# A two-layer decoder trunk in one kernel: order of the work between the first norm and the expert loop

## What is computed

```python
h = layer_norm(DN_ALPHA * h + mix, ln1_g[l], ln1_b[l])        # (xf - mu) * rsqrt(var + EPS) * g + b
scores = jax.nn.sigmoid(xf @ w_router)                        # 272 tokens (16 meta, 256 real), 64 experts
# sel = scores + bias; best 4 of 8 groups by their two best sums; best 8 experts of these
gates = gates / gates.sum(-1, keepdims=True) * ROUTE_SCALE
routed = sum over the chosen experts: gate * (silu(x @ w_gate) * (x @ w_up)) @ w_down
shared = (jax.nn.silu(xf @ ws_gate) * (xf @ ws_up)) @ ws_down
h = layer_norm(DN_ALPHA * h + routed + shared, ln2_g[l], ln2_b[l])
```

## Time and profile before

| | |
|---|---|
| device time, median of 3 runs | 1487.34 us |
| lowest and highest | 1483.96, 1491.04 us |
| profiled execution, span from first to last instruction | 1480.7 us |
| TensorE matmul busy | 1430.7 us, 97% |
| VectorE busy | 353.0 us, 24% |
| ScalarE busy | 254.0 us, 17% |
| GpSimd busy | 138.3 us, 9% |

### The profile page before, as it was taken

The page is one execution under the profiler, slowest core; times in us unless marked ns, Lnnn a source line. Parts: engine busy times, 40 slices in busy tenths (PEclk is TensorE's granted clock), DMA queues, the critical chain, the costliest instruction groups (busy, mean ns, idle before and its releaser), DMA issues. The chain is left out here.

```text
span 1480.7 us, 21355 instructions
## 1 busy us (share of the span) xinstructions
PE 1430.7 (97%) x8428; PEld 739.1 (50%) x8428; DVE 353.0 (24%) x1093; ACT 254.0 (17%) x608; POOL 138.3 (9%) x169
## 2 busy tenths in 40 slices
PE   8999999999999999999979999999999999999996
PEld 4755544444544454445437654444544554554552
DVE  0444551111111111111143435511111111111112
ACT  1243201111111111111122441011111111111110
POOL 2032111000000000000000221100000000000000
PEclk9999999999999999999989999999999999999998
DMA  9722429999999999999935224299999999999990
GB/s 331 299 97 86 172 78 380 409 407 396 400 400 402 394 400 407 406 393 399 346 139 199 94 106 171 78 388 405 410 417 415 412 413 414 409 413 414 413 398 33
DMA packets 103489, 471.66 MB, mean 319 GB/s; under 512 B 11744, under 2 KB 18080, under 8 KB 70544
## 3 DMA queue, kind: packets, MB, share of 16 engines
q1 hardware_dynamic: 91344, 442.32, 75.1%
q0 software_dynamic: 12096, 28.70, 5.5%
HBM read 484.91 MB, written 3.35 MB: 330 GB/s over the span
## 5 line engine op out<-in xcount | busy, mean ns | idle before, releaser
L614 PE MATMUL bank<-ring,region 128*64 128x256 f32 x4096 | 456.0, 381 | 1.7 <-issue 1.7
L614 PEld LDWEIGHTS bank<-ring,region 128*64 128x64 f32 x4096 | 296.9, 138 | 176.2 <-issue 39.7
L573 PE MATMUL bank<-region 128*128 128x512 f32 x512 | 267.5, 607 | 1.4 <-ACTq L1322 0.7
L652 PE MATMUL bank<-ring,region 128*64 128x512 f32 x1024 | 249.6, 608 | 2.4 <-ACT region L1141 1.4
L1532 DVE TENSOR_TENSOR region<-region,bank 128x256 f32<-128x256 f32 x64 | 27.0, 421 | 560.2 <-ACT region L1134 560.2
L1141 ACT ACTIVATE region<-bank 128x512 f32<-128x512 f32 x128 | 76.4, 597 | 474.6 <-PE bank L652 474.6
L1830 POOL DMA_INDIRECT region<-h_rows,rank_i x64 | 63.7, 995 | 919.7 <-DVE region L1511 863.8
L652 PEld LDWEIGHTS bank<-ring,region 128*64 128x64 f32 x1024 | 62.3, 136 | 162.9 <-issue 86.5
L573 PEld LDWEIGHTS bank<-region 128*128 128x128 f32 x512 | 78.1, 191 | 58.1 <-issue 54.9
L586 PEld LDWEIGHTS bank<-const,region 128*128 128x128 f32 x512 | 66.9, 195 | 69.2 <-ACT region L1125 42.7
L1134 ACT ACTIVATE region<-bank 128x256 f32<-128x256 f32 x64 | 24.6, 385 | 413.8 <-PE bank L614 413.8
(11 more groups left out here) (206 smaller groups left out, 847.6 us busy)
## 6 DMA issues: line engine op xcount, KB each, us to landing
ring<-in_w_gate_dram SPq DMA_DIRECT2D x64, 2048.0 KB, 10.4
ring<-in_w_up_dram SPq DMA_DIRECT2D x64, 2048.0 KB, 13.0
ring<-in_w_down_dram SPq DMA_DIRECT2D x64, 2048.0 KB, 9.1
ring<-in_w_in_dram SPq DMA_DIRECT2D x8, 2048.0 KB, 17.4
ring<-in_w_o_dram SPq DMA_DIRECT2D x4, 2048.0 KB, 11.0
ring<-in_w_in_dram SPq DMA_DIRECT2D x4, 1024.0 KB, 8.2
ln_par<-in_ln_g_dram POOLq DMA_DIRECT2D x4, 512.0 KB, 5.5
ln_par<-in_ln_b_dram POOLq DMA_DIRECT2D x4, 512.0 KB, 7.4
```

The costliest lines, as they stand in the source:

```text
L573: last = mm(bank[SUM_BANKS[n][half]][0:w, :], selg[:, u, t0:t0 + w], y_sb[:, u, half * 512:(half + 1) * 512], start=False, stop=stop, skip ...
L614: last = mm(bank[5][64 * e:64 * e + 64, part * F:(part + 1) * F], xgT[:, u, kk, 64 * e:64 * e + 64], w[:, e, kk, :], start=(kk == 0), stop ...
L652: last = mm(bank[6][64 * e:64 * e + 64, :], mo["h2"][:, j * 128 + 64 * e:j * 128 + 64 * e + 64], w[:, e, j, half * 512:(half + 1) * 512], ...
```

## The change

- `finish` moves from VectorE to GpSimd, for all chunks of the first norm. It stands there right behind the powers and ahead of the clearing of `score`.
- `xg` is cleared by ScalarE, as a copy of constants with scale 0, behind its last router sigmoid; a new semaphore, `rows_clear`, tells GpSimd. `moe_clear` now counts `score` alone.
- VectorE makes all eight list steps at once (`first_lists`), with `wait_ge` where `hold_here` stood, ahead of the maximum count and of all shared hidden values. These come in `round_`, behind `read_lists`.
- TensorE turns the lists ahead of opening the sums. Down product of chunk 1 stays ahead of the loop; those of chunk 2 and, in layer 0, chunk 0 go in four pieces into the first pair, where the scatters are in the others. `scattered` is raised by the last piece.

```diff
@@ -574,7 +575,7 @@
                               start=False, stop=stop, skip_group_check=True)
                 return last
 
-            def round_(l, r):
+            def round_(l, r, shared_piece=None):
 
                 g = l * ROUNDS + r
                 past = pe.snap(rounds_run)
@@ -625,11 +626,15 @@
                             pe.wait_ge(y_ready, g * 64 + p * 2)
                             pe.wait_ge(selg_ready, g * 32 + p)
                             scatter(l, 1 - u, 1, 0)
+                        elif shared_piece:
+                            shared_piece(0)
                         if not ends:
                             pe.wait_ge(xta_ready, g * 32 + p + 2)
                             turn_x(1 - u, 1)
                         if not opens:
                             scatter(l, 1 - u, 1, 1)
+                        elif shared_piece:
+                            shared_piece(1)
                         pe.wait_ge(h_ready, g * 32 + p + 1)
                         if not ends:
                             pe.wait_ge(xtb_ready, g * 32 + p + 2)
@@ -640,6 +645,8 @@
                             scatter(l, 1 - u, 2, 0)
                             if l == 0:
                                 scatter(l, 1 - u, 0, 0)
+                        elif shared_piece:
+                            shared_piece(2)
                         pe.wait_ge(ht_ready, g * 32 + p + 1)
                         pe.wait_ge(slot_in[base + 2], arrived)
                         w = ring[:, base + 2, :].rearrange("p (e j n) -> p e j n", e=2, j=2)
@@ -655,6 +662,8 @@
                             last.then_inc(y_done, 1)
                             if half == 0 and not opens:
                                 scatter(l, 1 - u, 2, 1).then_inc(scattered, 1)
+                            elif half == 0 and shared_piece:
+                                shared_piece(3).then_inc(scattered, 1)
 
                 two_pairs(0, first=True)
                 with pe.Fori(1, PAIRS // 2 - 1) as i:
@@ -1019,38 +1028,46 @@
                             mm(bank[b][:, :], k["alpha"], h_tok[:, n, half * 512:(half + 1) * 512], start=True, stop=False,
                                skip_group_check=True)
 
-                def shared_down(n):
+                def shared_down(n, pieces):
+
                     t0, w = CHUNKS[n]
                     pe.wait_ge(shared_ready, SHARED[l][n])
-                    if n == 0:
-                        parts = [(o, q * 256, 256) for q, o in enumerate(meta_quads(SUM_BANKS[0][0], 256))]
-                    else:
-                        parts = [(bank[b][0:w, :], half * 512, 512) for half, b in enumerate(SUM_BANKS[n])]
-                    for j in range(2):
+                    for at in pieces:
+                        if n == 0:
+                            j, parts = at, [(o, q * 256, 256) for q, o in enumerate(meta_quads(SUM_BANKS[0][0], 256))]
+                        else:
+                            j, half = at // 2, at % 2
+                            parts = [(bank[SUM_BANKS[n][half]][0:w, :], half * 512, 512)]
                         for o, c0, cols in parts:
                             last = mm(o, hsT[:, j, t0:t0 + w], wsd[:, j, c0:c0 + cols], start=False, stop=False,
                                       skip_group_check=True)
                     return last
 
+                pe.wait_ge(score_ready, SCORED[l])
+                if l == 0:
+                    pe.wait_ge(shared_sig, SHARED[l][0])
+                turn_lists(l * ROUNDS)
                 pe.wait_ge(h_ready_tok, NORM[(l, 0)][2])
-                pe.wait_ge(ws_down_in, l * 16 + 16)
                 open_sums(1)
                 turn_hidden(1)
                 open_sums(2)
                 turn_hidden(2)
-                shared_down(1)
-                pe.wait_ge(score_ready, SCORED[l])
-                turn_lists(l * ROUNDS)
+                pe.wait_ge(ws_down_in, l * 16 + 16)
+                shared_down(1, range(4))
                 if l == 0:
                     turn_hidden(0)
                     open_sums(0)
-                last = shared_down(2)
-                if l == 0:
-                    last = shared_down(0)
-                last.then_inc(scattered, 1)
                 hold_here(pe, count_ready, l + 1)
                 most = pe.value_load(count_i[0:1, 0:1], min_val=0, max_val=T)
-                round_(l, 0)
+                pe.wait_ge(shared_ready, SHARED[l][QUERIES[l][0] if l == 0 else 2])
+
+                def shared_piece(at):
+                    last = shared_down(2, [at])
+                    if l == 0 and at >= 2:
+                        last = shared_down(0, [at - 2])
+                    return last
+
+                round_(l, 0, shared_piece)
                 last_sums(l, 0, sums_done, SUMMED[l][SUM_ORDER[l][-1]])
                 with pe.If(most > CAP):
                     with pe.Fori(1, ROUNDS) as r:
@@ -1276,7 +1293,7 @@
 
                 def scores(ns, part):
                     act.wait_ge(router_done, l * 2 + part + 1)
-                    act.wait_ge(moe_clear, l * 2 + 2)
+                    act.wait_ge(moe_clear, l + 1)
                     for n in ns:
                         w = CHUNKS[n][1]
                         act.activation(rows3["score"][0:w, n, :], bank[7][0:w, n * E:(n + 1) * E], ACT.Sigmoid).then_inc(score_ready, 1)
@@ -1285,6 +1302,8 @@
                 scores(QUERIES[l][:-1], 0)
                 router_rows(144, T, 1)
                 scores([2], 1)
+                act.wait_ge(const_in, 16)
+                act.activation(mo["xg"], const[:, 0:2 * ROW], ACT.Copy, scale=0.0).then_inc(rows_clear, 1)
 
                 def shared_gate(n):
                     act.wait_ge(h_ready_tok, NORM[(l, 0)][1])
@@ -1432,15 +1451,11 @@
                     rows_to_features((l, 0), 0)
                 shift(l, 0, 1)
                 normalise(l, 0, 1)
-                if l == 0:
-                    finish(l, 0, 0)
                 stats(l, 0, 2)
                 rows_to_features((l, 0), 1)
                 shift(l, 0, 2)
                 normalise(l, 0, 2)
                 rows_to_features((l, 0), 2)
-                finish(l, 0, 1)
-                finish(l, 0, 2)
 
             def expert_norm(l):
 
@@ -1492,6 +1507,16 @@
                     dve.match_replace(left, eight, left, 0.0).then_inc(list_step, 1)
                     hold_here(dve, list_step, g * (CAP // 4) + 2 * j + 2)
 
+            def first_lists(l):
+
+                left, at = mo["left"][0:64, FIRST[l]:T], l * ROUNDS * (CAP // 4)
+                for j in range(CAP // 8):
+                    eight = mo["list"][0:64, 8 * j:8 * j + 8]
+                    dve.max(eight, left).then_inc(list_step, 1)
+                    dve.wait_ge(list_step, at + 2 * j + 1)
+                    dve.match_replace(left, eight, left, 0.0).then_inc(list_step, 1)
+                    dve.wait_ge(list_step, at + 2 * j + 2)
+
             def read_lists(g):
 
                 dve.wait_ge(list_turned, g + 1)
@@ -1516,7 +1541,8 @@
                     make_lists(l, g)
                 read_lists(g)
                 if shared_hidden:
-                    shared_hidden(0)
+                    for n in SHARED[l]:
+                        shared_hidden(n)
                 turned(0, 0)
                 read_gate(0, 0)
 
@@ -1752,20 +1778,17 @@
                         last = dve.tensor_tensor(o, o, u, ALU.mult)
                     last.then_inc(hid_ready, 1)
 
-                shared_hidden(1)
                 dve.wait_ge(chosen_turned, l + 1)
                 dve.scalar_tensor_tensor(mo["left"][0:64, lo:T], bank[4][0:64, lo:T], -1.0, k["iota_t"][0:64, lo:T],
                                          ALU.mult, ALU.mult).then_inc(left_ready, 1)
+                dve.wait_ge(left_ready, l + 1)
+                first_lists(l)
                 step(dve.tensor_reduce(mo["cmax"][0:1, :], bank[4][0:1, 448:512], AX, ALU.max))
                 after_steps()
                 dve.tensor_copy(count_i[0:1, :], mo["cmax"][0:1, :]).then_inc(count_ready, 1)
-                dve.wait_ge(left_ready, l + 1)
-                make_lists(l, l * ROUNDS, 0, 5)
-                shared_hidden(2)
-                make_lists(l, l * ROUNDS, 5)
                 hold_here(dve, count_ready, l + 1)
                 most = dve.value_load(count_i[0:1, 0:1], min_val=0, max_val=T)
-                round_(l, 0, False, shared_hidden if l == 0 else None)
+                round_(l, 0, False, shared_hidden)
                 with dve.If(most > CAP):
                     with dve.Fori(1, ROUNDS) as r:
                         round_(l, r, True)
@@ -1817,6 +1840,17 @@
                     pool.wait_ge(ln_var_ready, NORM[(l, ph)][n])
                     pool.tensor_tensor(ln_rstd[0:w, n:n + 1], ln_var[0:w, n:n + 1], half_pow[0:w, 0:1], ALU.pow)\
                         .then_inc(ln_rstd_ready, 1)
+
+            def finish(l, n):
+
+                rows = slice(0, CHUNKS[n][1])
```

(12 more changed lines are left out.)

1 line of the change is left out of this document (added).

## The result

The changed kernel takes 1491.87 us (median of 20 runs, 1489.81 to 1496.60), the kernel before 1488.05 us beside it (20 runs, 1481.12 to 1491.48). The ratio, taken over all the runs, is **1.0033, interval 1.0022 to 1.0044**: 4.9 us slower (the two medians lie 3.8 us apart), half of the 9.8 us forecast, and less than the 0.5% above which I had called it slower. The profiled execution took 1496.27 us with a span of 1494.3 us, so 2.0 us lie around the span.

A forecast was written before the change was run, and what follows sets the result against it. TensorE's work ahead of the expert loop and in the first pair sets the change: +2.75 us at high clock plus 7.05 us of clock falls, +9.8; with 6.6 us to the median, 1497.1 us; 8-in-10 range 1487 to 1502.

The forecast's parts named there:

- Part 1: GpSimd finishes of 2.4 us ahead of score clear: TensorE resumes 7.0 us later in layer 0, 2.3 in layer 1.
- The port pair: VectorE's two-input choice steps could each wait out a 2.4 us GpSimd finish; in this order they do not meet.
- Part 2: ScalarE clears the gather rows in 2.0 us after its last router sigmoid, with nobody waiting: cost nothing.
- Part 3: Eight list steps at once on VectorE, 0.98 us each; TensorE stands still 3.1 us in layer 0, 4.8 in layer 1.
- Part 4: Last shared down products in first expert pair: 16.44 us in layer 0, 15.88 in layer 1, instead of 17.01 and 18.34.
- The clock: Three TensorE standstills each bring a clock fall, 2.35 us apiece: 7.05 us; first pairs taken as free of falls.
- I add the difference to the median: Last step: the three-run median 1487.34 lies 6.6 us above the profiled span 1480.7; adding this gives 1497.1 us.
- Rival 1: TensorE's clock falls less often, two, one or no times: 1490 to 1494.7 us; chance 0.26.
- Rival 2: GpSimd's finishes are over when TensorE needs the router-sum copy: 1481.4 to 1486.1 us; chance 0.07.
- Rival 3: TensorE also stops at hidden transposes, and a fourth clock fall in row transposes: 1499 to 1501, or 1503 us; chance 0.09.

## Why the forecast came out as it did

**Part 1, the queue on GpSimd: mechanism right, size too large.** The clear was what ScalarE and TensorE waited for, shown by moving it alone. Less the 3.99 and 12.94 us by which the ruler's starts themselves lie later (180.69 and 930.05 against 176.70 and 917.11), TensorE's block of shared products started 5.5 us later than before and not 7.0 in layer 0, 1.3 and not 2.3 in layer 1. The term is the length of a finish: 2.00 us for the multiplication and 2.34 to 2.41 us for the addition in place, 2.2 in the mean. The range given, 1.27 to 2.54, held it; the straight line through the earlier trace rows joined two lines of code, and the multiplication lies below it. Six times 0.2 us are 1.2 of the 1.5 us; the other 0.3 is the hold-up by VectorE's normalisation, which did not come, for the first addition (183.26) starts right behind its multiplication (181.20 + 1.99 us).

The gaps were forecast at 6.5 and 1.9 us and measured 3.89 us and none. TensorE came to them later by itself, since its router sums, behind a wait of 2.44 us that the kernel before has too, ran at half clock this time. TensorE in the trace of before, in the changed kernel, and layer 1 of the kernel that clears the rows twice:

```profile
178.06 2.15 PE L949 MATMUL bank<-hT,wr 128*64 128x144 f32 x16 [2.44 <-DVE hT L1358]
```

```profile
182.06 3.66 PE L958 MATMUL bank<-hT,wr 128*64 128x144 f32 x16 [2.44 <-DVE hT L1377]
```

```profile
937.13 0.27 PE L965 MATMUL bank<-const,region 64*128 64x64 f32 x1 [1.19 <-ACT region L1091]
```

In that last kernel the same code ran these sums at the full clock, and the gaps are 5.40 and 1.19 us. So the 1.3 us of layer 1 can't be put down to the queue alone from the changed kernel's own trace: there the copy behind the clear and TensorE's slower work were both done at about 940.2. The other trace shows the queue's wait by itself.

**The port pair.** I said they would not meet in this order and the choice's first step took 0.36 us: right. In the order that lets them meet it took 2.10 us.

**Part 2.** 2.01 us against 2.0, nobody waited: right.

**Part 3.** A list step is 1.00 us, forecast 0.98; standstills 3.37 and 4.80 us, forecast 3.1 and 4.8. What I left out is that the half clock behind the first gap also delays the lists: the block takes 10.51 us and not 8.85, VectorE gets the turned choice that much later, and its first list step comes 12.4 us after TensorE's resumption and not 10.8.

**Part 4.** Layer 1: 15.94 us for the first pair, forecast 15.88. Layer 0: 18.74 us, forecast 16.44. Of the 2.30 us, 1.73 are clock (8.81 against 7.08 us). The other 0.57 is a term that I missed: the down product of the meta tokens is twice eight matmuls of 256 columns, the scatter in its place in the other pairs once eight.

```profile
241.04 1.58 PE L1042 MATMUL bank<-region 128*128 128x512 f32 x10
...
244.42 1.68 PE L1042 MATMUL bank<-region 128*128 128x512 f32 x10
...
258.99 0.63 PE L570 MATMUL bank<-region 128*16 128x256 f32 x8
```

The first two rows, merged, hold two matmuls of 512 columns and eight of 256 each; the last row is all that a pair's scatters do for the meta tokens.

**The clock, in the trace.** I took three falls at 2.35 us, 7.05. Inside the ruler four cost time on the path (those in the router sums only shortened the gaps behind them): 1.66 (L973), 1.40 (L1028) and 1.7 us (L615) in layer 0, and about 2.6 us behind the list wait of layer 1, together 7.4. The sum was right by luck: the falls were shorter and there was one more, in the first pair of layer 0, which I had declared free of it. It was wrong to think that only a standstill ahead brings one.

**The clock, over all executions.** Here the forecast's largest term fails. It charges 7.05 us of half clock to the new order, against a trace of before whose clock falls nowhere between 780 and 950 us nor between 60 and 200. But the mean granted clock is 0.9872 over the 100 executions of before on record and 0.9861 over the 20 of the changed kernel. A straight line through the 100 (span against clock) gives some 1.2 us for 0.001, so, as an estimate, the clock is 1.3 us of the 4.9 (0.5 to 1.8, by which group of before it is set against). At the same clock the changed kernel is 3.8 us longer, against 2.75 forecast.

**Sum and base.** 9.8 forecast, 8.0 in the region of the traces, 4.9 by the ratio. The first difference is mostly the finishes. The second is the step "I add the difference to the median": it takes the profiled execution for a typical one. That execution shows no fall of the clock between 60 and 200 us nor between 780 and 950 us, while the median of the same kernel is some 5.5 us above it (1488.05 against 1480.7 + 1.9, and 1486.29 against 1480.80); by the estimate above, most of the clock loss that I charged to the new order is matched by what the old one loses in other executions. The measured 1491.87 us lies in the 8-in-10 range of 1487 to 1502, but below the forecast's own 1494.7 to 1500: that the wider range held it owes something to luck. Rival 1 (the clock falls less often) gave 1490 to 1494.7 and holds the measured time. Its mechanism is not what the trace shows, where the falls came; but its result, little clock loss on balance, is what the executions show. Rival 2 fell: the finishes were not hidden. Rival 3's waits for the hidden values did not come; its fourth fall did.

## What to carry to other kernels

When work moves onto another engine's queue, look first at the smallest thing that is queued behind it: here a memset of 0.26 us, and moving it was worth 8 us, while with it in front the engine on which the finishes ran made no difference that could be measured (0.9979 and 0.9983). Producing something early on one engine gives nothing until its consumer has other work to do meanwhile; and the cover taken from one wait must be counted at the next, lists, hidden values and gather in turn. A standstill of TensorE also costs what runs at half clock behind it, here 3.7 us behind 3.37 and 4.80 us of waiting. And before the difference of two traces is called the effect of a change, look where each lies among the executions of its kernel: here the traces differ by 13.6 us and the kernels by 4.9.

## What the runs showed of the hardware

- TensorE's granted clock goes to 1.2 GHz not only behind idle time. At 76 to 80 us of the changed kernel its matmuls fill 4.00 of 4.00 us and the clock is 0.50 all the same; in two traces of the kernel before it is 1.00 there. A wait of 2.44 us ahead of the router sums is followed by the full clock in the trace of before (2.15 us) and by half the clock in that of the changed kernel (3.66 us). Nine of the twelve traces that are not of the kernel before show a fall between 74 and 83 us, seven one between 816 and 840 us. What decides it is open, and two traces of before are too few to say that it falls less often there.
- The spread from run to run goes with it: in the changed kernel executions with spans of 1488.0 to 1488.6 us have a mean clock of 0.987 to 0.988, those of 1494.3 to 1494.8 us 0.982 to 0.983. On 1442 us of busy TensorE 0.005 of the clock is 7 us.
- GpSimd's two-operand operation of 1024 columns takes as long on 16 partitions as on 128: the addition in place 2.40 and 2.34 us, the multiplication into another tile 1.99 us on both. Whether the 0.35 us between the two come from the operation or from the place of its output isn't shown.
